# Layer 1 (SSD): the outputs are transposed before they are gated, and the sums of squares go through GpSimd and TensorE

## The reference, cut to what matters

```python
    y = y + d_skip.astype(f32).reshape(SSD_GROUPS, SSD_HPG)[..., None] * x
    y = y.reshape(bsz, l, SSD_DINNER) * jax.nn.silu(z)
    yg = y.reshape(bsz, l, SSD_GROUPS, SSD_DINNER // SSD_GROUPS)
    yg = yg * lax.rsqrt(jnp.mean(yg * yg, axis=-1, keepdims=True) + NORM_EPS)
    y = yg.reshape(bsz, l, SSD_DINNER) * w_norm.astype(f32)
    out = y.astype(h.dtype) @ w_out
```

## Time and profile before

| | |
|---|---|
| median of 3 runs | 1468.57 us (1468.32 to 1468.98) |
| the profiled execution | 1467.13 us |
| its span in the trace | 1465.1 us |
| mean granted PE clock | 0.99 of full speed |
| layer 1's events | from about 655 us to the end |

### The profile page before, as it was taken

How to read it: one execution, slowest core, us unless ns; L and a number is a source line. 1 busy time by engine, 2 the same in 40 slices (tenths; PEclk the granted TensorE clock), 3 DMA queues, 4 the chain that set the end, 5 groups by cost and what they waited for, 6 DMA issues and landing times. The chain is left out here.

```text
span 1465.1 us, 32433 instructions
## 1 busy us (share of the span) xinstructions
PE 1401.1 (96%) x12082; PEld 1174.4 (80%) x12082; DVE 1162.2 (79%) x2591; ACT 832.4 (57%) x1877; POOL 233.1 (16%) x424
## 2 busy tenths in 40 slices
PE   6999998999999899998999999999999999999987
PEld 6999897777888689987978888877777777787765
DVE  5566787777878987889896998986879688588786
ACT  5755645485556455556566754654556365555553
POOL 5010202011321100121110220120012110000003
PEclk9999999999999999999999999999999999999999
DMA  7485647356585445377845844752675674554463
GB/s 214 140 256 152 215 113 228 93 184 177 146 239 163 122 131 162 91 175 209 262 127 165 249 137 138 233 152 64 201 224 150 180 207 117 173 168 154 135 195 65
DMA packets 284454, 245.83 MB, mean 168 GB/s; under 512 B 33240, under 2 KB 251452, under 8 KB 283628
## 3 DMA queue, kind: packets, MB, share of 16 engines
q1 hardware_dynamic: 274204, 209.36, 48.1%
q0 software_dynamic: 10096, 34.41, 8.9%
HBM read 183.02 MB, written 65.00 MB: 169 GB/s over the span
## 5 line engine op out<-in xcount | busy, mean ns | idle before, releaser
L1515 PE MATMUL bank<-h,w 128*128 128x268 f32 (+1 forms) x4752 | 830.0, 329 | 9.8 <-ACT w L894 5.0
L1515 PEld LDWEIGHTS bank<-h,w 128*128 128x128 f32 x4752 | 695.5, 190 | 86.5 <-issue 12.7
L910 DVE TENSOR_TENSOR w<-w_raw,w 128x1024 fp32r<-128x1024 f32 x132 | 160.9, 1219 | 38.5 <-ACT w L894 38.4
L879 PE MATMUL bank<-s_w_out,s_yt_hi 128*128 128x512 f32 (+2 forms) x544 | 168.1, 398 | 1.7 <-DVE s_ys L2661 1.0
L894 ACT ACTIVATE w<-w_raw 128x1024 fp32r<-128x1024 f32 x132 | 138.8, 1052 | 15.7 <-DMA w_raw<-in_ssd_w_in_dram 9.6
L1593 DVE SCALAR_TENSOR_TENSOR conv<-before_conv,cw,conv 128x260 f32<-128x260 f32 (+2 forms) x216 | 125.3, 580 | 4.2
L879 PEld LDWEIGHTS bank<-s_w_out,s_yt_hi 128*128 128x128 f32 (+2 forms) x544 | 95.9, 180 | 28.1 <-issue 2.1
L879 PE MATMUL bank<-s_w_out,s_yt_lo 128*128 128x512 f32 x240 | 94.7, 395 | 0.0
L879 PE MATMUL bank<-g_w_out,g_ot_hi 128*128 128x512 f32 (+2 forms) x288 | 92.6, 409 | 1.6 <-DVE g_ot_lo L2179 1.6
L2424 ACT ACTIVATE s_decay<-s_decay,t_ac 128x128 f32<-128x128 f32 (+1 forms) x288 | 85.4, 379 | 1.2
L2743 ACT ACTIVATE s_yt_hi<-bank 128x512 fp32r<-128x512 f32 (+1 forms) x36 | 20.1, 557 | 115.1 <-PE bank L2734 115.0
(11 more groups left out here) (259 smaller groups left out, 2435.1 us busy)
## 6 DMA issues: line engine op xcount, KB each, us to landing
w_raw<-in_ssd_w_in_dram SPq DMA_DIRECT2D x80, 512.0 KB, 4.1
w_raw<-in_gla_w_in_dram SPq DMA_DIRECT2D x48, 512.0 KB, 4.8
s_decay<-kept_acd SPq DMA_DIRECT2D x32, 512.0 KB, 6.5
w_raw<-in_ssd_w_out_dram SPq DMA_DIRECT2D x30, 512.0 KB, 4.4
s_chunk<-kept_sq SPq DMA_DIRECT2D x32, 384.0 KB, 4.8
kept_sq<-stage SPq DMA_DIRECT2D x80, 134.0 KB, 4.3
g_chunk<-kept_gq SPq DMA_DIRECT2D x32, 320.0 KB, 4.3
kept_sq<-stage SPq DMA_DIRECT2D x40, 256.0 KB, 4.9
```

Of the source, the lines that this page charges most:

```text
L879: last = pe.matmul(bank[0:r, :], yt[a][:, k, 0:r], wo[:, b, 512 * half:512 * half + 512], start=(k + a + b == 0), stop=(k == tiles - 1 and ...
L910: dve.tensor_tensor(self.part(i, 1), self.raw(i), hi, ALU.subtract).then_inc(self.w_lo, 1)
L1515: last = pe.matmul(bank[:, 0:n], w[:, p.tile % 2, a, k, :], h[:, b, k, c:c + n], start=(i == 0), stop=(i == len(terms) - 1))
```

## The change

1. `gates` is gone: z is not transposed, nor are the sample answers. At its place in `step` and `ssd` stands `turn`: PE transposes the raw, ungated rows y (L2734's transposes, now behind `y_summed`) into the output bank.
2. `norm` on DVE: the transposed outputs in PSUM times z with its channels on partitions, into a new SBUF tile `og` (128x4x128).
3. `highs`, at the old place of `turn`: ACT rounds `og` to the high part, DVE subtracts for the low part, both from SBUF. `square` on ACT now waits for that low part and squares `og` in place. GpSimd folds the four squared blocks to one in two additions (`pool_fold`).
4. `sums`, one event later, between scan and turn: four matmuls of one column on PE (one for step 0) sum over the partitions into a column of SU, ACT copies it out, GpSimd makes mean and root. They wait for `s_new` of the scan just issued.
5. Step 0: `first_out` transposes its rows right after its scan and DVE keeps them in SBUF; answers (8 columns, not turned) are added there.
6. z is loaded by a task of its own (`z_in`, 2 events ahead), behind `products`; its buffer comes free with the gating. Waits follow: the next scan waits for `gated` of the event before instead of its low part, and `inputs` no longer waits for step 0's gating.

```diff
-        ssd = [("decay", 1), ("scan", 0), ("fill", 0.5), ("lows",),
-               ("weight", 3, 1), ("fill", 0.5), ("gates", 0), ("load", 2), ("lows",), ("fill", 0.3), ("norm", 0),
-               ("inputs", 1), ("products_late", -1), ("weight", 0, 0), ("fill", 0.5), ("lows",), ("fill", 0.5),
-               ("products_first", -1), ("turn", 0), ("square", 0), ("weight", 1, 0), ("r_add", -2), ("r_in", -1),
+        ssd = [("decay", 1), ("scan", 0), ("fill", 0.5), ("lows",), ("sums", -1),
+               ("weight", 3, 1), ("fill", 0.5), ("turn", 0), ("load", 2), ("lows",), ("fill", 0.3), ("norm", 0),
+               ("inputs", 1), ("products_late", -1), ("z_in", 2), ("weight", 0, 0), ("fill", 0.5), ("lows",), ("fill", 0.5),
+               ("products_first", -1), ("highs", 0), ("square", 0), ("weight", 1, 0), ("r_add", -2), ("r_in", -1),
...
-        step = [("decay", 1), ("scan", 0), ("fill", 0.6), ("lows",), ("weight", 1), ("fill", 0.5), ("gates", 0),
-                ("load", 2), ("lows",), ("fill", 0.4), ("norm", 0), ("inputs", 1), ("products", -1),
+        step = [("decay", 1), ("scan", 0), ("fill", 0.6), ("lows",), ("sums", -1), ("weight", 1), ("fill", 0.5), ("turn", 0),
+                ("load", 2), ("lows",), ("fill", 0.4), ("norm", 0), ("inputs", 1), ("products", -1), ("z_in", 2),
...
+    def pool_fold(self, pool, u, s):
+
+        o, og, n = oev(u, s), self.t["og"], step_cols(s)[1]
+        pool.wait_ge(self.rows.squared, self.rows.squares[("square", 1, u, s)])
+        pool.tensor_tensor(og[:, 0:2, 0:n], og[:, 0:2, 0:n], og[:, 2:4, 0:n], ALU.add).then_inc(self.folds, 1)
+        pool.wait_ge(self.folds, 2 * o + 1)
+        pool.tensor_tensor(og[:, 0, 0:n], og[:, 0, 0:n], og[:, 1, 0:n], ALU.add).then_inc(self.folds, 1)
...
-            pe.wait_ge(self.yt_lo, self.issued[("scan", u, s)]["turn"])
+            self.turn_read(pe, e)
+        pe.wait_ge(self.sums_kept, self.issued[("scan", u, s)]["sums"])
...
+    def turn_outputs(self, pe, u, s):
+        n = step_cols(s)[1]
+        pe.wait_ge(self.y_summed, ev(u, s) + 1)
+        for j in range(4):
+            last = pe.transpose(self.y_bank(u, s)[:, j * n:(j + 1) * n], self.t["y"][0:n, j * P:(j + 1) * P],
+                                self.m["ident"][0:n, 0:n])
+        last.then_inc(self.y_turned, 1)
...
+    def pe_turn(self, pe, u, s):
+        if self.late(u, s):
+            pe.wait_ge(self.gated, oev(u, s))
+        elif self.issued[("turn", u, s)]["sums"]:
+            pe.wait_ge(self.sums_kept, self.issued[("turn", u, s)]["sums"])
+        self.turn_outputs(pe, u, s)
+
+    def dve_gate(self, dve, u, s):
...
+        if o:
+            dve.wait_ge(self.summed, o)
+        dve.tensor_tensor(t["og"][:, :, 0:n], y, z, ALU.mult).then_inc(self.gated, 1)
...
+    def act_square(self, act, u, s):
+
+        t, o, n = self.t, oev(u, s), step_cols(s)[1]
+        act.wait_ge(self.yt_lo, o + 1)
+        before = self.rows.squares[("square", 1, u, s)] - 1
+        act.wait_ge(self.rows.squared, before)
+        act.activation(t["og"][:, :, 0:n], t["og"][:, :, 0:n], ACT.Square).then_inc(self.rows.squared, 1)
+
+    def pe_sums(self, pe, u, s):
+
+        o, n = oev(u, s), step_cols(s)[1]
+        pe.wait_ge(self.folds, 2 * (o + 1))
+        pe.wait_ge(self.s_new, self.issued[("sums", u, s)]["scan"])
+        for j in range(0, n, SUB):
+            k = min(SUB, n - j)
+            last = pe.matmul(self.SU[j:j + k, 0:1], self.t["og"][:, 0, j:j + k], self.m["ones"][:, 0:1], start=True, stop=True)
+        last.then_inc(self.summed, 1)
```

More of the change, by code:

```diff
@@ L200, in stage @@
             if 0 <= e < len(EVENTS):
-                outputs = L == 1 and (name.startswith("r_") or name in ("gates", "norm", "turn", "square", "products"))
+                outputs = L == 1 and (name.startswith("r_") or name in ("sums", "norm", "turn", "highs", "square", "products"))
                 u, s = (OUTPUTS if outputs else EVENTS)[e]
@@ L235, in skeleton @@
                ("fill", 0.3), ("lows",), ("weight", 2, 0), ("fill", 0.3), ("r_square", -1), ("r_out", -2), ("fill", 0.3)]
-        first = [("decay", 1), ("meta",), ("scan", 0), ("fill", 0.6), ("lows",), ("fill", 0.4), ("load", 2), ("lows",),
-                 ("fill", 0.4), ("inputs", 1), ("products", -1), ("fill", 0.4), ("lows",), ("spread", 0),
+        first = [("decay", 1), ("meta",), ("scan", 0), ("fill", 0.6), ("lows",), ("sums", -1), ("fill", 0.4), ("first_out",),
+                 ("load", 2), ("lows",),
+                 ("fill", 0.4), ("inputs", 1), ("products", -1), ("z_in", 2), ("fill", 0.4), ("lows",), ("spread", 0),
@@ L268, in beside_samples @@
                         tasks.extend([("sample", 1, u, 2 * s + at[0]), ("answer", u, 2 * s + at[0])])
-                elif name in ("decay", "scan", "load", "inputs"):
+                elif name in ("decay", "scan", "load", "inputs", "z_in"):
                     stage(1, name, e + at[0])
-                elif not (name == "products" and s == 1):
+                elif not (name in ("products", "sums") and s == 1):
                     stage(1, name, o + at[0])
@@ L2262, in __init__ @@
                                                          for x in ("ck_in", "acb_in", "z_in", "back"))
-        self.issued, count = {}, dict.fromkeys(("inputs", "spread", "scan", "gates0", "turn", "products"), 0)
+        self.issued, count = {}, dict.fromkeys(("inputs", "spread", "scan", "sums", "products"), 0)
         for name, *at in W.plan.order:
@@ L2267, in __init__ @@
                 self.issued[(name, u, s)] = dict(count)
-                if name == "gates" and s == 0:
-                    count["gates0"] += 1
-                elif name in count and not (name == "turn" and self.late(u, s)):
+                if name in count:
                     count[name] += 1
-            elif name == "meta":
+            elif name in ("meta", "first_out"):
                 self.issued[(name, *at)] = dict(count)
@@ L2394, in root @@
         q = slice(o % 4, o % 4 + 1)
-        pool.wait_ge(self.rows.squared, self.rows.squares[("square", 1, u, s)])
+        pool.wait_ge(self.sums_kept, o + 1)
         if o >= 4:
@@ L2696, in pe_gates @@
[L2696 to L2718 removed]
+            y, z = self.y_of(u, s), t["zc"][:, q % 2, :, 0:n]
@@ L2723, in act_square @@
         if o >= 4:
             act.wait_ge(self.rooted, o - 3)
-        before = self.rows.squares[("square", 1, u, s)] - 1
-        act.wait_ge(self.rows.squared, before)
-        act.activation(self.m["junk"][0:n, :], self.outputs(s)[0:n, :], ACT.Square,
-                       accum_out=t["ysum"][0:n, o % 4:o % 4 + 1]).then_inc(self.rows.squared, 1)
-    def pe_turn(self, pe, u, s):
-        o, n = oev(u, s), step_cols(s)[1]
-        pe.wait_ge(self.gated, o + 1)
-        for j in range(4):
-            last = pe.transpose(self.y_bank(u, s)[:, j * n:(j + 1) * n], self.outputs(s)[0:n, j * P:(j + 1) * P],
-                                self.m["ident"][0:n, 0:n])
-        last.then_inc(self.y_turned, 1)
```

183 lines of the change are left out of this document (94 added, 89 removed).

## The result

| | before | after |
|---|---|---|
| median | 1468.44 us (1468.05 to 1468.98, 4 runs) | 1538.28 us (1536.26 to 1540.26, 4 runs) |
| ratio to before | | 1.0477 (95% interval 1.0463 to 1.0491) |
| profiled execution, span | 1467.1, 1465.1 us | 1536.6, 1534.9 us |
| PE busy / not busy in the span | 1401.1 / 64.0 us | 1416.1 / 118.8 us |
| mean granted PE clock | 0.99 | 0.97 |

The change makes the kernel 4.8% slower: 70 us, where 21.5 had been forecast and 1508 us was the upper end of the range. The direction was right and the size was not.

The account below looks back on a forecast made before the run. PE, 96% busy, was taken as the bound: its work plus its waits. Group 0 +5.1, group 1's ordinary events +1.7, late events and tail +14.7 made +21.5 us, forecast 1490.0 us, range 1467 to 1508.

Parts of the forecast that it names:

- ACT's square behind DVE's low part: On ACT, the square's new wait for DVE's low part, in most events 0.7 us: costed at nothing.
- PE's saved work: On PE, z's and the answers' turning gone (14.7 us), new one-column matmuls added (5.3 us): net gain 9.4 us.
- PE's wait for `y_summed`: At the turn PE stands for DVE's sixth scan operation: 22.1 us group 0, 3.8 group 1's ordinary events, 18.1 late.
- What is given back: Later PE waits swallowed: 3.8 us group 0, 2.4 late; stalls after DVE idled for late weight tiles: 6.9 off.
- the three banks of the pieces cover it: ACT's next piece is delayed, but buffering hides it: nothing; if not, 1 us for each of some 8 events.
- adds nothing of its own: On PE, `sums` waits for `s_new` half a fill before the turn; PE leaves the turn at the same moment: 0.
- The folds: GpSimd's two additions per output, 0.74 and 0.46 us, with over 4 us until `sums`: taken as 0, other end 20.
- GpSimd would lose a collision: Where GpSimd and DVE exclude one another, one row showed GpSimd waiting; used for taking 0 us of DVE delay.
- PE's work deciding: Rival: stalls replace later PE waits, only a third of the late stage's stall stays; 1461 us, chance 0.13.
- the late stage alone: Rival: half of group 0's stalls are absorbed, late events cost as summed; 1479 us, chance 0.17.
- Folds holding DVE: Rival: GpSimd's additions block DVE's ports, 10 us, plus 5 for ACT behind DVE; 1505 us, chance 0.15 including late roots.
- Sums that come late for the folds: Rival: GpSimd's additions or root come late, some 3 us at four late outputs; 1502 us, chance 0.15 shared with DVE blocking.

Follow-up runs that it names:

- b_wait_sum: The kernel before with one more wait: PE turns z only after `y_summed`, in every event; 1519.05 us, ratio 1.0342.
- squares' own tile: The changed kernel with ACT's squares written to a separate tile, not waiting for DVE's low part, z single-buffered; 1522.54 us, ratio 1.0373.
- a_best: The changed kernel with sums, turn and gating behind the inputs, late sums in the output's own bank, squares in a separate tile; 1491.91 us, ratio 1.0167.
- b_wait_filled: The kernel before with z's turning waiting for `y_summed` in the five late events, three useless 512-column matmuls ahead of each wait; 1485.67 us, ratio 1.0117.
- b_wait_late: The kernel before with z's turning waiting for `y_summed` in the five late events alone, PE idle meanwhile; 1493.35 us, ratio 1.0169.

## Why the prediction was right and wrong

The forecast of +21.5 us failed in two terms that it had put at nothing: the clock behind PE's stalls, and ACT's square behind DVE's low part. A third, PE's saved work, was put too high.

- **PE's wait for `y_summed`** was the right mechanism, and its size was right: 44.0 us summed, 47.1 us alone on the chip, each late event within 0.3 us. What is given back was about right too: 30.9 us net forecast, 34.9 us more of PE standing in `b_wait_sum`.
- **The clock** is the largest step that was missing. The sum took PE's work behind each stall at its old duration. With the wait alone the same work took 19.1 us more. In after an estimate is 24 us (15.0 more busy, though 9.4 less work); by half of the added time at half clock (68 us against 24) it is 22. The filled wait shows that it is the clock: 7.7 us come back. The earlier trace rows could have warned. The 18 matmuls behind the wait of 2.14 us took 3.95 us there; at full clock the kernel before takes 2.46 us for 18 of the same:

```profile
728.07 2.46 PE L1515 MATMUL bank<-h,w 128*128 128x268 f32 x18
```

The 0.96 of the late stretch in the earlier trace rows is no such warning: its clock fell at 1459.7 us, when PE's last matmul (1455.8) was over.

- **ACT's square** behind DVE's low part was costed at 0, with 8 us if its cover was gone; it is 19 us alone and 15 to undo. The failed step is "the three banks of the pieces cover it". The reasoning looked at ACT's share and at the piece next in line, not at what lies behind it: the sample decays for which DVE waits, and so the next scan, and the roundings for which PE waits. ACT's wait came to 43.7 us over 32 outputs. The 0.7 us read "in most events" hold for half of them: in the kernel before the low part already ended over 0.9 us behind the high part in 16 of 32, 41.2 us in all.
- **The sums' wait "adds nothing of its own"** was about right. In after PE waits there in 18 events, up to 6.3 us, but sums and turn together are 55.9 us once ACT's wait is gone, against 52.1 us of `b_wait_sum` at turn and scan. The prediction also counted nothing for the old waits ahead of the scans, since PE would stand for the same time at the new place; that fits too. Turn and sums were moved together in the experiments, so what the sums' wait costs by itself stays open. (For u = 3 `s_new` comes one operation later than the order given for the scan says: there DVE makes the skip term first, in the third late event L2638 at 1421.30 us and L2646 at 1421.90.)
- **The folds** were priced at 0 with 20 as the upper end: 5 us in after. Their durations in after were as estimated (medians 0.74 and 0.46 us; 0.81 and 0.80 in `a_best`, where they collide). The argument that GpSimd would lose a collision, from one row, was wrong: in the rows of `a_best` the one that starts first wins, and in the row of before it was DVE that had started first. That after escapes it is due to the square's wait.
- **PE's saved work** was credited with 9.4 us. A like saving of 8.6 us gave 2.
- **The rivals.** PE's work deciding, and the late stage alone, are refuted. Folds holding DVE (1505 us) happens in `a_best` (18.1 us of DVE's time), hardly in after (2.9). Sums that come late for the folds do happen, for 6.6 us in after, 5.5 of them in the late events, and the folds' whole price is 5 us instead of that rival's 12. The 43 us at the sums are another wait, for `s_new`.

Put together by the single runs: 50 for the wait with its clock, 19 for the square, 5 for the folds, less 2 to 9 for PE's work, make 65 to 72 us; measured 70. The parts act on one another, so that this sum is a consistency, not a proof. By place it is less tidy: from the first late scan to the end the wait alone takes 92.6 us and after 102.6; of these 10 us 1.5 are gone with the squares' own tile and 2.9 without the folds. What makes the rest is open. The order of the turn, worth 27 to 31 us, is another cut through the same loss and isn't added.

## What to carry to other kernels

Price a stall of a nearly always busy PE twice: once for the time it stands and once for the work behind it at half clock; here the second was over half of the first (19 and 35 us). Look in the trace of before for a group of matmuls right behind a stall and compare it with the same group elsewhere. When an instruction gets a new wait, follow its engine's queue to what other engines wait for there; an engine at 56% busy gave no cover. Undoing one wait can bring on a collision that it had kept away, as the squares' own tile did. When the last wait in a loop is another engine's backlog, less work on the busiest engine can turn into waiting, as most of the 8.6 us of transposes did.

## What the runs showed of the hardware

- After PE stood for 5.53 us its next 128-column transposes ran at half pace (four in 1.06 us instead of 0.60) and its 512-column products at 0.63 us instead of 0.40. Behind the wait of 3.73 us the transposes were still fast and the clock was at 0.50 from 1448 us on, some 1.2 us after the wait; behind waits of 2.32 and 2.53 us it did not fall (all in `b_wait_sum`).
- Matmuls that do no work, put into five waits, made a kernel 7.7 us faster (`b_wait_filled` against `b_wait_late`).
- In `a_best` a GpSimd addition of two SBUF operands that was running held a DVE operation on two SBUF operands back by 0.54 us in the two rows shown, and a running DVE operation stretched the GpSimd one from 0.46 to 1.33 us.
